# A diffusion block's feed-forward part: weight slots, the last two down-projection blocks, and where the turns stand

## The reference, cut to what matters

```python
def _swiglu(h, w_gate, w_up, w_down):
    return (jax.nn.silu(h @ w_gate) * (h @ w_up)) @ w_down
...
        mix_x = jnp.concatenate([pool_x, attn_x], axis=-1) @ w_out[layer]
...
        x = x + g_m[:, None] * mix_x
        hf = _rmsnorm(x, norm_ffn[layer]) * (1.0 + sc_f[:, None]) + sh_f[:, None]
        x = x + g_f[:, None] * _swiglu(hf, w_gate[layer], w_up[layer], w_down[layer])

    return _rmsnorm(x, final_norm)
```

## Time and profile before

| what | value |
|---|---|
| median of 3 runs | 2949.62 us (2948.25 to 3105.07) |
| profiled execution: its time, its span | 2945.67 us, 2944.1 us (slowest core, 7) |
| spans of the cores | 2930.6 to 2944.1 us |
| PE, DVE, ACT, POOL busy | 93%, 36%, 25%, 5% of the span |
| granted clock of PE, mean of core 7 | 0.967 |

### The profile page before, as it was taken

The page is one execution under the profiler, slowest core; times in us unless marked ns, Lnnn a source line. Parts: engine busy times, 40 slices in busy tenths (PEclk is TensorE's granted clock), DMA queues, the critical chain, the costliest instruction groups (busy, mean ns, idle before and its releaser), DMA issues.

```text
span 2944.1 us, 39881 instructions; the slowest of 8 cores (2930.6 to 2944.1 us)
## 1 busy us (share of the span) xinstructions
PE 2745.3 (93%) x15444; PEld 1351.3 (46%) x15444; DVE 1060.2 (36%) x1689; ACT 724.0 (25%) x1235; POOL 149.9 (5%) x275
## 2 busy tenths in 40 slices
PE   3799988898998999999999999699999999999995
PEld 2444446665544444444444444244444444444442
DVE  2337666775332133124124116341142142133136
ACT  3313677787524000000000012142000000000012
POOL 1002320000000000000000000000000000000000
PEclk7799999999999999999999999799999999999998
DMA  9881137877433444443444444843444443443443
GB/s 220 212 159 29 30 104 216 272 259 182 119 71 58 78 82 75 74 88 63 77 81 76 75 83 88 252 72 54 76 79 72 75 90 67 77 80 71 74 86 134
DMA packets 40170, 311.29 MB, mean 106 GB/s; under 512 B 5168, under 2 KB 5424, under 8 KB 5680
## 3 DMA queue, kind: packets, MB, share of 16 engines
q0 software_dynamic: 25008, 205.71, 37.2%
q1 hardware_dynamic: 14976, 103.02, 11.0%
HBM read 475.58 MB, written 16.79 MB: 167 GB/s over the span
## 4 chain that ended last, share of the span: by engine, by line
PE 86%; DMA 6%; DVE 3%; issue 2%; ACT 2%; POOL 0%; DVEq 0%; another core or an unknown queue 0%; SPq 0%; ACTq 0%; POOLq 0%
PE ps L883 41%; PE ps L936 21%; PE ps L407 9%; PE ps L839 5%; PE ps L703 4%; PE ps L689 4%; DMA out<-arena 2%; DMA arena<-wada 1%; DMA arena<-x 1%; DMA arena<-wadat 1%; ACT arena L361 1%; DVE arena L632 1%; DVE arena L943 1%; DVE arena L710 1%; DMA arena<-wo 1%
## 5 line engine op out<-in xcount | busy, mean ns | idle before, releaser
L883 PE MATMUL ps<-arena 128*128 128x512 bf16 x5632 | 1224.1, 380 | 12.3 <-ACT arena L871 4.4
L883 PEld LDWEIGHTS ps<-arena 128*128 128x128 bf16 x5632 | 552.2, 98 | 682.1 <-issue 22.9
L936 PE MATMUL ps<-arena 128*128 128x512 bf16 x2816 | 609.1, 379 | 0.0
L888 DVE TENSOR_TENSOR arena<-ps,arena 128x512 bf16<-128x512 f32 x176 | 121.8, 692 | 1093.1 <-PE ps L883 1084.7
L887 ACT ACTIVATE arena<-ps 128x512 f32<-128x512 f32 x176 | 105.0, 597 | 1546.6 <-PE ps L883 1546.6
L936 PEld LDWEIGHTS ps<-arena 128*128 128x128 bf16 x2816 | 275.7, 98 | 332.1
L819 DVE TENSOR_TENSOR arena<-ps,arena 128x512 f32<-128x512 f32 x320 | 221.2, 691 | 322.9 <-PE ps L936 233.2
L407 PE MATMUL ps<-arena 128*128 128x512 bf16 x1312 | 302.7, 389 | 5.8 <-DVE arena L393 5.8
L692 ACT ACTIVATE arena<-ps 128x1024 bf16<-128x1024 f32 x288 | 276.9, 1022 | 75.5 <-PE ps L689 67.0
L839 PE MATMUL ps<-arena 128*128 128x512 bf16 x1024 | 233.0, 391 | 31.3 <-DVE arena L819 27.0
L820 DVE TENSOR_TENSOR arena<-arena 128x512 f32<-128x512 f32 x320 | 221.7, 693 | 71.5 <-DMA arena<-x 38.6
(11 more groups left out here) (84 smaller groups left out, 954.0 us busy)
## 6 DMA issues: line engine op xcount, KB each, us to landing
arena<-wgu POOLq DMA_DIRECT2D x88, 1024.0 KB, 8.4
arena<-wadat SPq DMA_DIRECT2D x64, 1024.0 KB, 6.3
arena<-wd POOLq DMA_DIRECT2D x32, 1408.0 KB, 9.8
arena<-x POOLq DMA_DIRECT2D x16, 1024.0 KB, 17.8
arena<-wada POOLq DMA_DIRECT2D x8, 2048.0 KB, 31.0
arena<-x SPq DMA_DIRECT2D x16, 1024.0 KB, 9.6
arena<-wo POOLq DMA_DIRECT2D x16, 1024.0 KB, 9.0
out<-arena SPq DMA_DIRECT2D x16, 1024.0 KB, 6.9
```

What stands on the lines that cost most here:

```text
L883: s.op("pe", [lambda e, kc=kc, g_=g_, b=b: e.matmul(bank(b), lhsT=w4[:, g_, kc, :], rhs=cat_ap(kc, *cr), start=(kc == 0), stop=(kc == 15)) ...
L888: s.op("dve", lambda e: e.tensor_tensor(out=actT.ap[:, fl, ar[0]:ar[1]], in0=bank(ub_), in1=sgb.ap, op=ALU.mult), reads=[ps(ub_), sgb.k()] ...
L936: s.op("pe", [lambda e, fl=fl, t=t, w3=w3: e.matmul(bank(t), lhsT=actT.ap[:, fl, t * 128:(t + 1) * 128], rhs=w3[:, fl, :], start=(fl == 0) ...
```

## The change

Weight slots: besides A and B (`ring`) there is C in pass 0, in the third row of `GB`, which holds the final norm's weights and is now loaded only at the end of pass 0. In pass 1 there are D0 to D3 instead, in the columns of `CP` and `QT` that belonged to pass 0's tokens, and X, which is D2 and D3 together, takes the last `wd` slab of either pass. A list `items3` names the slot of every slab beforehand. A slot is free once its reader is done (`ring3_done`), and then `ring3_load` issues as many of the next slabs as find their slot free, in the order of the list. A limit `gate` holds some loads back.

Last two blocks: in `q` = 3 the blocks `n` = 2 and 3 are done tile by tile, 22 matmuls for each tile, and `finish` follows each tile: ACT scales columns 1280 to 2047, DVE does columns 0 to 1279 in one multiply, POOL multiplies ACT's part by the weights, SP stores.

Turns: those of token half 0 stand between the last tiles of the projection, those of half 1 between and inside the gate/up units, and three units run ahead of half 1 instead of two.

```diff
-        xn3 = [buf(o + 4096 + i * 4096, [128, D], BF16) for i in range(4)]; o += 22528
+        xn3 = [buf(o + 6144 + i * 4096, [128, D], BF16) for i in range(4)]; o += 22528
...
-        s.dma("sp", GB.ap[:, 2, :], fn_d.partition_broadcast(128), "g_sm0", writes=[GB.k(2)])
...
+            def load(self, src, W):
+                if self.flat is not None:
+                    s.dma("pool", self.flat.ap[:, 0:W], src, self.group, writes=[self.keys(0, W)])
+                    return
+                b_, j0 = self.rows
+                nr = W // 1024
+                s.dma("pool", b_.ap[:, j0:j0 + nr, 0:1024], src[:, 0:nr * 1024].rearrange("p (a b) -> p a b", b=1024), self.group, writes=[self.keys(0, nr * 1024)])
+                if W % 1024:
+                    s.dma("pool", self.at(nr * 1024, W % 1024), src[:, nr * 1024:W], self.group + "r", writes=[self.keys(nr * 1024, W % 1024)])
+        SA, SB = [Slot("AB"[i], ["AB"[i]], "g_r3_%d" % i, flat=ring[i]) for i in range(2)]
+        SC = Slot("C", ["C"], "g_r3_c", flat=buf(GB.off + 16384, [128, 4096], BF16))
+        SD = [Slot("D%d" % i, ["D%d" % i], "g_r3_d%d" % i, rows=((CP, CP, QT, QT)[i], (0, 4, 0, 4)[i])) for i in range(4)]
+        SX = Slot("X", ["D2", "D3"], "g_r3_x", rows=(QT, 0))
         items3 = []
+        rot = {"i": 0}
+
+        def put(kind, k, slots):
+            items3.append((kind, k, slots[rot["i"] % len(slots)]))
+            rot["i"] += 1
+
         for p in range(2):
-            items3 += [("wo", k) for k in range(8)]
+            three = [SA, SB, SC] if p == 0 else [SA, SB] + SD
+            if p == 1:
+                for k, sl in enumerate([SD[0], SD[1], SB, SA, SD[2], SD[3], SD[0], SD[1]]):
+                    items3.append(("wo", k, sl))
+            else:
+                for k in range(8):
+                    put("wo", k, three)
             for q in range(4):
-                items3 += [("wgu", 11 * q + f) for f in range(11)] + [("wd", 4 * q + n) for n in range(4)]
+                for f in range(11):
+                    put("wgu", 11 * q + f, three)
+                for n in range(4):
+                    items3.append(("wd", 4 * q + n, SX if (q == 3 and n == 3) else (SA, SB)[n % 2]))
         r3 = {"next": 0, "cons": 0}
+        held = {}
 
         def ring3_load():
-            i = r3["next"]
-            if i >= len(items3):
-                return
-            kind, k = items3[i]
-            src = {"wo": wo_d, "wgu": wgu_d, "wd": wd_d}[kind][k]
-            W = 5632 if kind == "wd" else 4096
-            s.dma("pool", ring[i % 2].ap[:, 0:W], src, "g_r3_%d" % (i % 2), writes=[ring[i % 2].k((0, W))])
-            r3["next"] += 1
+            while r3["next"] < len(items3):
+                kind, k, sl = items3[r3["next"]]
+                if any(r in held for r in sl.need) or (r3["gate"] is not None and r3["next"] >= r3["gate"]):
+                    return
+                src = {"wo": wo_d, "wgu": wgu_d, "wd": wd_d}[kind][k]
+                sl.load(src, 5632 if kind == "wd" else 4096)
+                for r in sl.need:
+                    held[r] = r3["next"]
+                r3["next"] += 1
 
         def ring3_take():
             i = r3["cons"]
             r3["cons"] += 1
-            return ring[i % 2]
+            assert i < r3["next"], i
+            return items3[i][2]
+
+        def ring3_done(sl):
+            for r in sl.need:
+                del held[r]
+            ring3_load()
+
+        FIRST = 8 + 4 * 15
+        r3["gate"] = FIRST - 1
...
-        def transposed(c0, st_, jh, b0):
+        def transposed(c0, st_, jps, b0, nb):
             cr = (c0 + st_ * 512, c0 + (st_ + 1) * 512)
-            for jp in range(4):
-                b = b0 + jp
+            for jp in jps:
+                b = b0 + jp % nb
...
+                if g_ == 0:
+                    for f in between:
+                        f()
...
+        def down(t, n, b, slot, squares):
+            s.op("pe", [lambda e, fl=fl: e.matmul(bank(b), lhsT=actT.ap[:, fl, t * 128:(t + 1) * 128], rhs=slot.at(fl * 512, 512), start=(fl == 0), stop=(fl == 10)) for fl in range(11)],
+                 reads=[slot.keys(0, 5632), actT.k(None, (t * 128, (t + 1) * 128))], writes=[ps(b)])
+            evac_residual(b, t, n, 1, squares)
+
+        NV = 1280
+
+        def finish(p, t):
+
+            r0 = p * 1024 + t * 128
+            rs = rstd_of(t)
+            lo, hi = x1.ap[:, t, 0:NV], x1.ap[:, t, NV:D]
+            s.op("act", lambda e: e.activation(out=hi, in_=hi, func=AF.Copy, scale=rs), reads=[x1.k(t, (NV, D)), ("rs3", t)], writes=[x1.k(t, (NV, D))])
+            s.op("dve", lambda e: e.scalar_tensor_tensor(out=lo, in0=lo, scalar=rs, in1=GB.ap[:, 2, 0:NV], op0=ALU.mult, op1=ALU.mult),
+                 reads=[x1.k(t, (0, NV)), ("rs3", t), GB.k(2)], writes=[x1.k(t, (0, NV))])
+            s.op("pool", lambda e: e.tensor_tensor(out=hi, in0=hi, in1=GB.ap[:, 2, NV:D], op=ALU.mult), reads=[x1.k(t, (NV, D)), GB.k(2)], writes=[x1.k(t, (NV, D))])
+            s.dma("sp", out_d[r0:r0 + 128, :], x1.ap[:, t, :], "g_st%d" % (t % 2), reads=[x1.k(t)])
...
             outproj_part(c0, 3, 0, sl0, range(4, 8))
-            ring3_load()
-            outproj_part(c0, 3, 1, sl1, range(4, 8))
-            ring3_load()
-            transposed(c0, 0, 0, 0)
-            transposed(c0, 0, 1, 0)
+            ring3_done(sl0)
+            for t in range(4, 8):
+                outproj_part(c0, 3, 1, sl1, [t])
+                if t < 6:
+                    transposed(c0, 0, (2 * t - 8, 2 * t - 7), 0, 4)
+                elif t == 6:
+                    transposed(c0, 0, (4, 5, 6, 7), 0, 4)
+            ring3_done(sl1)
             normalize(1)
             for q in range(4):
                 f0 = 0
                 if q == 0:
-                    sl0, sl1 = ring3_take(), ring3_take()
+                    sl = [ring3_take() for _ in range(3)]
                     unit["i"] = 0
-                    gate_up(c0, 0, 0, sl0)
-                    gate_up(c0, 1, 0, sl1)
-                    transposed(c0, 1, 0, 4)
-                    transposed(c0, 1, 1, 4)
-                    gate_up(c0, 0, 1, sl0)
-                    ring3_load()
-                    gate_up(c0, 1, 1, sl1)
-                    ring3_load()
-                    f0 = 2
+
+                    def turns(*jps):
+                        return lambda: transposed(c0, 1, jps, 6, 2)
+
+                    gate_up(c0, 0, 0, sl[0])
+                    gate_up(c0, 1, 0, sl[1])
+                    turns(0, 1)()
+                    gate_up(c0, 2, 0, sl[2], between=[turns(2, 3), turns(4)])
+                    turns(5, 6, 7)()
+                    for i in range(3):
+                        gate_up(c0, i, 1, sl[i])
+                        ring3_done(sl[i])
+                    f0 = 3
                 for fl in range(f0, 11):
                     slot = ring3_take()
                     for st_ in range(2):
                         gate_up(c0, fl, st_, slot)
+                    ring3_done(slot)
+                last = q == 3
+                if last:
+                    if p == 0:
+                        s.dma("sp", GB.ap[:, 2, :], fn_d.partition_broadcast(128), "g_sm0", writes=[GB.k(2)])
+                    r3["gate"] = None
                     ring3_load()
-                for n in range(4):
+                for n in range(2 if last else 4):
                     slot = ring3_take()
-                    w3 = slot.ap.rearrange("p (k c) -> p k c", k=11)
                     for t in range(8):
-                        s.op("pe", [lambda e, fl=fl, t=t, w3=w3: e.matmul(bank(t), lhsT=actT.ap[:, fl, t * 128:(t + 1) * 128], rhs=w3[:, fl, :], start=(fl == 0), stop=(fl == 10))
-                                    for fl in range(11)],
-                             reads=[slot.k(), actT.k(None, (t * 128, (t + 1) * 128))], writes=[ps(t)])
-                        evac_residual(t, t, n, 1, q == 3)
-                    ring3_load()
-            for t in range(8):
-                rs = rstd_of(t)
-                s.op("dve", lambda e, t=t, rs=rs: e.scalar_tensor_tensor(out=x1.ap[:, t, :], in0=x1.ap[:, t, :], scalar=rs, in1=GB.ap[:, 2, :], op0=ALU.mult, op1=ALU.mult),
-                     reads=[x1.k(t), ("rs3", t), GB.k(2)], writes=[x1.k(t)])
-                s.dma("sp", out_d[c0 + t * 128:c0 + (t + 1) * 128, :], x1.ap[:, t, :], "g_st%d" % (t % 2), reads=[x1.k(t)])
-                if p == 0 and t >= 1:
-                    x1_load(1, t - 1)
+                        down(t, n, t, slot, last)
+                    ring3_done(slot)
+                if last:
+                    sl = [ring3_take(), ring3_take()]
+                    for t in range(8):
+                        for i in range(2):
+                            down(t, 2 + i, (2 * t + i) % 8, sl[i], True)
+                        if t == 7:
+                            ring3_done(sl[0])
+                            ring3_done(sl[1])
+                        finish(p, t)
```

(24 more changed lines are left out.)

24 lines of the change are left out of this document (20 added, 4 removed).

## The result

The changed kernel takes 2970.59 us (median of 4, 2970.36 to 2971.12) beside a kernel before of 2948.25 and 2949.62: a ratio of 1.0074, interval 1.0049 to 1.0098, so 22 us slower. The forecast was 10.8 us slower: the sign and the five waits were right, the size was half of what was measured.

The account below looks back on a forecast made before the run. TensorE (PE), busy 93% of the span, was taken as the bound, so only its idle places could be won. 12.0 + 31 + 5.4 us won, 59.2 lost: 10.8 slower than 2949.62, so 2960, range 2937 to 2987.

Parts of the forecast that it names:

- the five waits: Block changes, three in pass 0, two in pass 1: PE idles 10.5 us for `wd`, 9.1 for `wgu`.
- P0: Pass 0, first output projection matmul to first `gate_up`: forecast -3.9 us.
- F0: Pass 0, first `gate_up` to last `wd` matmul: forecast +53.2 us together with F1.
- F1: Pass 1, first `gate_up` to last matmul: forecast +53.2 us together with F0.
- B: Boundary, pass 0's last `wd` matmul to pass 1's first `gate_up`: forecast -33.2 us, 31 of it from the boundary term.
- end: Last matmul to end of the span, norm and store: forecast 5.4 us won.
- Turns between matmul groups: Output projection and first `gate_up`: waits for ACT offset by what the third slot hides, 0 plus or minus 3 us a pass.
- Weight waits added: Five loads needing the slot of the group just ended: idle PE and lower clock, 59.2 us lost, bounds 55.3 to 68.4.
- Weight waits removed: PE's waits for `wo` and `wgu` and the slower matmuls after two: 12.0 us won, bounds 10 to 12.
- (1): Rival: added load waits are hidden after all, only gains left, 2901, or 2881 with gains at upper end; chance 0.08.
- (2): Rival: loads issued together share the queue, the awaited one lands with its followers, 62 us, 3022; chance 0.07.
- (3): Rival: POOL and DVE don't hinder each other in the norm, period 6.1, 62.1 us won in all, 2947; chance 0.10.

Follow-up runs that it names:

- e9: e6 with `wd` 14 instead of `wd` 15 in X and the gate one item earlier; no ratio from this run, 0.9829 when run again.
- e10: e9 with the change's turns between the matmul groups; ratio 0.9818 [0.9749, 0.9887].
- e1: The changed kernel with the slot used longest ago taken for every load, nothing else changed; 2904.09 us, ratio 0.9872.
- e6: e1 with the turns put back where they were before the change; ratio 0.9841.
- e7: The changed kernel with, at the five places, the loads behind the awaited one held until 7 us after its landing; ratio 1.0102.
- e2: The changed kernel with, at the five places, the loads behind the awaited one held until it has landed; ratio 1.0090.
- e4: The changed kernel with the final norm's multiply on DVE alone, nothing of it on ACT and POOL; 2980.00 us, ratio 1.0134.
- e8: e4 with three `wo` loads held until DVE has multiplied tile 6; ratio 1.0083.

## Why the prediction was wrong

The forecast by stages was: P0 -3.9 (one `wo` wait and the clock behind it), F0 and F1 +53.2 (59.2 less 6.0 of `wgu` waits), B -33.2 (31 and the other `wo` wait), end -5.4; +10.7. Measured: +1.2, +62.3, -31.0, -5.5; +27.0. The two sums lie 16.3 us apart: 5.1 in P0, 9.1 in F0 and F1, 2.2 in B.

**Failed: "Turns between matmul groups: 0, plus or minus 3 a pass."** They cost 6.6 us between e9 and e10, and 9 by the ratios of e1 and e6: 3.3 in P0, 3.6 in B, the rest, less certain, in the first `gate_up` block. The wait was named (ACT delivers 4 us later; 5.4 measured in P0, 3.9 in B) but set off against the third slot, which hides nothing there: without the turns' move P0 and B are shorter by 3.3 and 3.6.

**Failed on half of the cores: "Weight waits added ... Sum: 3 x 12.4 + 2 x 11.0 = 59.2 us."** On cores 1, 3, 5 and 6, F0 and F1 stand 59.3 us above e1's median, as forecast, clock included. On the four others they stand 70.2 above it (67.7 above the same cores of e1, which wait for `wd` 15 too). The landing was taken from loads in a kernel where little else moved; e7 shows that the partner's loads lengthen it. The metric is the slowest core, so the longer wait counts. The bound of 68.4 was nearly it, but for the wrong reason.

**Failed, small: "I cost it at nothing" of `wd` 15 in X.** On the same four cores its last piece landed 20.0 to 20.4 us after its issue behind `wd` 14. On core 4 that is 22.6 us after the block's end (1785.14 + 21.94 = 1807.08 to 1829.71), where the forecast had 20.1 and PE asks after 21.4. It cost 1.2 to 1.7 us of waiting and some clock. e9 removes it.

**Failed, small: "Weight waits removed: 12.0 us."** In P0 2.1 of 3.9 us were won (123.1 to 121.0 in e9, with the former turns): the lower clock after a `wo` wait, read on core 7, isn't there on most cores. In F0 and F1 4.3 of 6.0 were won (1846.0 to 1841.7 in e9).

**Right.** The five places. The time lies inside the stated 2937 to 2987. The boundary: 159.0 to 125.9 in e9, with the former turns, is 33.1 against 33.2; that it fits to 0.1 is luck, since cores 0 to 5 of the kernel before have a further `wo` wait of 1.8 to 3.3 us there that core 7, which the forecast was read from, has not. The end: 27.4 us, as forecast, but two errors cancel: on core 4 the first tile keeps DVE for 8.4 us (2905.87 to 2914.22) instead of 6.1, since PE hands over its second bank 2.4 us after the first, and each later tile takes 6.91 instead of 7.2. POOL's multiply: 2.16 was measured against 2.0, but only 1.7 of it fall beside DVE's next operations; the estimate of 1.7 and a period of 6.9 that the prediction sets beside its own was nearer. The clock after an idle stretch: on cores 1, 3, 5 and 6 the five stretches are 49.4 of the 59.3 us, so 2.0 us of lower clock for each against 1.9.

**The rivals.** (1) fell: all five waits are there. (2) fell as it was put: a core's own followers don't delay the awaited load (core 5 had one right behind and waited 10.7; e2's early cores hardly gain); the partner's followers do, by 6 to 10 us in all. The words of the Trainium skill that it was weighed against stand in "DMA: Bandwidth & Descriptors" under "Two DMAs through the same engine are not ordered"; they say that descriptors start in order, not that they land in order, so that the first lands first is what the earlier trace rows show and not the page. (3) fell: L882 at 1.51 is the exclusion, and e4 and e8 show that the split wins nothing.

## What to carry to other kernels

Write out for each load which group frees its slot; if it is the group that has just ended, the whole landing is idle time, and taking the slot used longest ago avoids it (59 us here). Price a load that PE waits for as the slowest core sees it, with its partner's loads beside it. Before work is taken off a queue's engine or given to it, look at which transfers it releases earlier or later: here the multiply on POOL was worth only the delay that it gave three loads.

## What was not expected of the hardware

Two cores of a pair slow each other's loads: 144 instead of 184 GB/s with the DMA engines 89% and 98% busy, and a wait of 13.2 instead of 10.7 us for the same slab. Three loads of 1024 KB beside a chain of stores and loads stretched its step from 9.6 to 16.7 us, which cost 9.6 us at the boundary (B 137.6 against 128.0).
